# A two-block hybrid layer: the delta rule on raw keys and queries, with their norms as factors of the tokens

## What is computed

```python
qkv = silu(causal_depthwise_conv(gdn_qkv, conv_w))          # h @ w_in, first 3072 columns
qa, ka, va = split(qkv)                                      # 8 heads of 128 each
qa, ka = l2_normalize(qa), l2_normalize(ka)                  # x * rsqrt(sum(x*x) + 1e-6)
beta = sigmoid(gdn_b);  g = -exp(a_log) * softplus(gdn_a + dt_bias)
# S_t = exp(g_t) S_{t-1} + beta_t k_t (v_t - exp(g_t) S_{t-1}^T k_t)^T ;  o_t = S_t^T q_t / sqrt(128)
oa = gated_delta_rule(qa, ka, va, beta, g)
oa = oa * rsqrt(mean(oa * oa) + 1e-6)                        # per token and head
oa = oa * gdn_norm_w * silu(gdn_z)
u_a = oa @ w_branch_a
```

## Time and profile before

| what | value |
|---|---|
| time, median of 3 runs | 1242.67 us (1242.46 to 1242.71) |
| span of the profiled execution | 1240.9 us |
| PE busy | 1218.7 us, 98% |
| DVE busy | 748.4 us, 60% |
| ACT busy | 611.1 us, 49% |
| POOL busy | 95.7 us, 8% |
| mean DMA rate | 181 GB/s |
| chain that ended last | PE 90%, DVE 4%, ACT 3%, issue 1%, DMA 1% |
| conv region | 0 to 167 us |

### The profile page before, as it was taken

How to read it: one execution, slowest core, us unless ns; L and a number is a source line. 1 busy time by engine, 2 the same in 40 slices (tenths; PEclk the granted TensorE clock), 3 DMA queues, 4 the chain that set the end, 5 groups by cost and what they waited for, 6 DMA issues and landing times.

```text
span 1240.9 us, 16520 instructions
## 1 busy us (share of the span) xinstructions
PE 1218.7 (98%) x6566; PEld 1022.1 (82%) x6566; DVE 748.4 (60%) x1008; ACT 611.1 (49%) x898; POOL 95.7 (8%) x129
## 2 busy tenths in 40 slices
PE   8899999999999999999999999999999999999997
PEld 8788888888878888888888888788897778888886
DVE  5668885665576656556455555667565646565654
ACT  5566454544424556444444444564444445466443
POOL 0010000179300000000000000000000000000000
PEclk9999999999999999999999999999999999999999
DMA  8646555576644544655666585466544656464662
GB/s 258 210 140 192 165 182 159 145 214 186 184 142 131 172 129 142 215 189 171 209 181 202 190 296 199 154 208 201 168 138 151 204 170 204 125 218 163 207 206 100
DMA packets 141101, 224.00 MB, mean 181 GB/s; under 512 B 10097, under 2 KB 60849, under 8 KB 140001
## 3 DMA queue, kind: packets, MB, share of 16 engines
q1 hardware_dynamic: 138576, 212.25, 54.6%
q0 software_dynamic: 2128, 9.64, 2.2%
q10 hardware_dynamic: 320, 1.06, 0.2%
HBM read 218.20 MB, written 4.72 MB: 180 GB/s over the span
## 4 chain that ended last, share of the span: by engine, by line
PE 90%; DVE 4%; ACT 3%; issue 1%; DMA 1%; POOL 0%; SPq 0%; POOLq 0%; ACTq 0%
PE acc L1941 62%; PE acc L1920 9%; PE acc L1922 5%; PE aux L1812 3%; PE aux L2186 2%; PE acc L1873 2%; DVE lo_w L1283 1%; PE aux L2162 1%; PE acc L1932 1%; ACT hi_w L902 1%; PE aux L1992 1%; DVE cv L1397 1%; PE aux L2052 1%; DMA x_in<-in_x 0%; PE aux L2155 0%
## 5 line engine op out<-in xcount | busy, mean ns | idle before, releaser
L1283 DVE TENSOR_TENSOR lo_w<-raw_w,hi_w 128x1024 fp32r<-128x1024 f32 x379 | 462.4, 1230 | 346.5 <-ACT hi_w L902 345.1
L902 ACT ACTIVATE hi_w<-raw_w 128x1024 fp32r<-128x1024 f32 x379 | 394.7, 1057 | 267.8 <-PE acc L1941 218.8
L1941 PE MATMUL acc<-hi_w,h_both 128*128 128x512 f32 (+1 forms) x1632 | 520.2, 391 | 1.2 <-DVE lo_w L1283 0.8
L1941 PEld LDWEIGHTS acc<-hi_w,h_both 128*128 128x128 f32 x1632 | 304.7, 188 | 65.6 <-issue 3.9
L1941 PE MATMUL acc<-lo_w,h_both 128*128 128x512 f32 (+1 forms) x816 | 314.6, 385 | 0.0
L1920 PE MATMUL acc<-h_both,hi_w 128*128 128x512 f32 x576 | 204.5, 399 | 2.4 <-DVE lo_w L1283 2.4
L1941 PEld LDWEIGHTS acc<-lo_w,h_both 128*128 128x128 f32 x816 | 153.6, 188 | 28.1
L1922 PE MATMUL acc<-h_both,lo_w 128*128 128x256 f32 x576 | 160.8, 279 | 0.0
L1920 PEld LDWEIGHTS acc<-h_both,hi_w 128*128 128x128 f32 x576 | 108.2, 188 | 28.3 <-DVE lo_w L1283 1.6
L1922 PEld LDWEIGHTS acc<-h_both,lo_w 128*128 128x128 f32 x576 | 108.6, 189 | 0.1
L1941 PE MATMUL acc<-hi_w,m_hi 128*128 128x512 f32 x224 | 87.5, 390 | 0.0
(11 more groups left out here) (348 smaller groups left out, 1246.4 us busy)
## 6 DMA issues: line engine op xcount, KB each, us to landing
raw_w<-in_w_in SPq DMA_DIRECT2D x283, 512.0 KB, 3.8
raw_w<-in_w_out SPq DMA_DIRECT2D x64, 512.0 KB, 4.8
raw_w<-in_w_branch_a SPq DMA_DIRECT2D x16, 512.0 KB, 4.6
raw_w<-in_w_branch_b SPq DMA_DIRECT2D x16, 512.0 KB, 4.7
raw_w<-in_cmp_k_w SPq DMA_DIRECT2D x8, 512.0 KB, 4.3
raw_w<-in_cmp_v_w SPq DMA_DIRECT2D x8, 512.0 KB, 4.9
x_in<-in_x SPq DMA_DIRECT2D x8, 256.0 KB, 8.4
x<-in_x POOLq DMA_DIRECT2D x1, 2048.0 KB, 9.6
```

The lines of the kernel that those rows point to most:

```text
L902: act.activation(hi_w[slot][:, 0:n], raw_w[no % RAW_SLOTS][:, 0:n], ACT.Copy).then_inc(*hi_ready.event(no))
L1283: dve.tensor_tensor(lo_w[slot][:, 0:n], raw_w[no % RAW_SLOTS][:, 0:n], hi_w[slot][:, 0:n].bitcast(F32), ALU.subtract).then_inc(*lo_ready.e ...
L1941: i = pe.matmul(to[:, t, 0:group.cols], x[at], w[:, k], start=first and k == 0 and m == 0, stop=last and k == n - 1 and m == 2)
```

## The change

q and k are no longer normalised. The silu writes them straight to `q_t` and `k_t` (channels x tokens, the form that `gram` and `delta` read), `conv_back` still transposes them, but only for the sums of squares and, for k, to fill `k_tok` for the first 128 tokens. `qk_flip`, `qk_out`, the scalings on DVE and the tile `q_tok` go. With r the root factor of k per token and head, three factors are made on POOL (`k_scale`, two ticks ahead of v's tokens for half 0): `k_v` = beta r for v's tokens, `k_low` = -beta r r in place of `nbeta`, `k_beg` = beta r r exp(gcum) in place of `beg`. The norm of q and the factor 1/sqrt(128) go into the epsilon of the norm behind the delta rule (`q_eps`), as a third instruction of its root on POOL. Waits follow: v's `token_out` on DVE waits for `k_scale`, `gram` for the silus, `conv_back` for ACT's square or copy, `delta` for the copy of k.

```diff
-    at(26, "beta_gcum")
+    at(27, "k_scale", 0)
+    at(END[("conv", "k", 1, 1)] + 7, "k_scale", 1)
...
-            if part != "v":
-                at(c + 8, "qk_flip", part, h)
-                at(c + 9, "qk_out", part, h)
...
-        small = place("small", [P, 400], F32)
+        small = place("small", [P, 480], F32)
...
# POOL
             def token_out(part, h):
-                if part != "v":
-                    pool.wait_ge(*dve_did.after("ssq", part, h))
-                    root(rnorm, ssq, 1.0, ("rnorm", part, h), SCALE if part == "q" else None)
+                if part == "q":
+                    pool.wait_ge(*dve_did.after("ssq", "q", h))
+                    pool.tensor_scalar(q_eps[h], q_ssq[h], EPS / SCALE ** 2, EPS * EPS / SCALE ** 2, ALU.mult,
+                                       ALU.add).then_inc(*pool_did.event("q_eps", h))
+                if part == "k":
+                    pool.wait_ge(*dve_did.after("ssq", "k", h))
+                    root(k_r[h], k_ssq[h], 1.0, ("k_r", h))
+
+            def k_scale(h):
+                pool.wait_ge(*act_did.after("eg"))
+                pool.wait_ge(*pool_did.after("k_r", h))
+                r = tiles(k_r[h], QUAD)
+                by_v, low, by_beg = (tiles(x, HEADS)[:, :, quad(h)] for x in (k_v, k_low, k_beg))
+                link(pool.tensor_tensor(by_v, tiles(beta, HEADS)[:, :, quad(h)], r, ALU.mult))
+                link(pool.tensor_tensor(low, by_v, r, ALU.mult))
+                link(pool.tensor_tensor(by_beg, low, tiles(eg, HEADS)[:, :, quad(h)], ALU.mult))
+                pool.tensor_scalar(low, low, -1.0, None, ALU.mult).then_inc(*pool_did.event("k_scale", h))
...
             def delta_norm(h):
                 pool.wait_ge(*dve_did.after("delta_ssq", h))
-                root(rnorm, ssq, 1.0 / P, ("delta_rnorm", h))
+                pool.wait_ge(*pool_did.after("q_eps", h))
+                link(pool.tensor_scalar(rnorm, ssq, 1.0 / P, None, ALU.mult))
+                link(pool.tensor_tensor(rnorm, rnorm, q_eps[h], ALU.add))
+                pool.tensor_tensor(rnorm, rnorm, half[:, 0:NT * QUAD], ALU.pow).then_inc(
+                    *pool_did.event("delta_rnorm", h))
...
# ACT
             def conv_silu(part, h):
                 act.wait_ge(*dve_did.after("conv", part, h))
-                if (part, h) != ("q", 0):
-                    act.wait_ge(*pe_did.after("conv_back", *before_conv(part, h)))
-                act.activation(sil[:], cv[:], ACT.Silu).then_inc(*act_did.event("silu", part, h))
+                if (part, h) == ("v", 1):
+                    act.wait_ge(*pe_did.after("conv_back", "v", 0))
+                act.activation(silu_of(part, h), cv[:], ACT.Silu).then_inc(*act_did.event("silu", part, h))
...
-            def qk_out(part, h):
-                act.wait_ge(*pe_did.after("qk_flip", part, h))
...
+                if part == "k":
+                    act.activation(k_tok[:, 0, quad(h)], aux[:, 2].rearrange("p (i c) -> p i c", c=P),
+                                   ACT.Copy).then_inc(*act_did.event("k_tok", h))
...
# DVE
-                dve.tensor_scalar(nbeta, beta, -1.0, None, ALU.mult)
...
-            def beta_gcum():
-                dve.wait_ge(*act_did.after("eg"))
-                dve.tensor_tensor(beg, beta, eg, ALU.mult).then_inc(*dve_did.event("beg"))
...
             def token_out(part, h):
                 if part == "v":
                     dve.wait_ge(*pe_did.after("conv_back", part, h))
+                    dve.wait_ge(*pool_did.after("k_scale", h))
...
                 dve.wait_ge(*act_did.after("sq", part, h))
-                if (part, h) != ("q", 0):
-                    dve.wait_ge(*pool_did.after("rnorm", *before_qk(part, h)))
-                dve.tensor_reduce(tiles(ssq, QUAD), sq[:], AXX, ALU.add).then_inc(*dve_did.event("ssq", part, h))
-                dve.wait_ge(*pool_did.after("rnorm", part, h))
-                if part == "q" and h:
-                    dve.wait_ge(*pe_did.after("qk_flip", "q", 0))
-                for t in range(NT):
-                    to = q_tok[:, t] if part == "q" else k_tok[:, t, quad(h)]
-                    last = dve.tensor_tensor(to, aux[:, 2 + t].rearrange("p (i c) -> p i c", c=P),
-                                             over_cols(rnorm[:, t * QUAD:(t + 1) * QUAD]), ALU.mult)
-                last.then_inc(*dve_did.event("token_out", part, h))
+                to = (q_ssq if part == "q" else k_ssq)[h]
+                dve.tensor_reduce(tiles(to, QUAD), sq[:], AXX, ALU.add).then_inc(*dve_did.event("ssq", part, h))
...
# PE
             def conv_back(part, h):
+                reader = {"q": (act_did, "sq", "q", h), "k": (act_did, "k_tok", h), "v": (dve_did, "token_out", "v", h)}
                 for b in (2, 3):
-                    take(b, (dve_did, "token_out", part, h))
+                    take(b, reader[part])
...
-            def qk_flip(part, h):
...
             def gram(h, t):
...
-                pe.wait_ge(*act_did.after("qk_out", "k", h))
+                for part in "qk":
+                    pe.wait_ge(*act_did.after("silu", part, h))
```

More of the change, by code:

```diff
@@ L466, in build @@
         ba = bit(NT * 16)
-        beta, nbeta, g, gcum, ngcum, eg, beg = (bit(NT * HEADS) for _ in range(7))
+        beta, g, gcum, ngcum, eg = (bit(NT * HEADS) for _ in range(5))
+        k_v, k_low, k_beg = (bit(NT * HEADS) for _ in range(3))
         tail, sp0, sp1, nexp = bit(HEADS), bit(NT * HEADS), bit(NT * HEADS), bit(HEADS)
+        q_ssq, k_ssq, q_eps, k_r = ([bit(NT * QUAD) for _ in range(2)] for _ in range(4))
         ssq, rnorm = bit(NT * QUAD), bit(NT * QUAD)
@@ L664, in over_cols, with silu_of @@
             return ap.unsqueeze(2).broadcast_to([P, ap.shape[-1], m])
+        silu_to = {"q": q_t, "k": k_t}
+        def silu_of(part, h):
+            return silu_to[part][:, quad(h)] if part in silu_to else sil[:]
         conv_order = [(p, h) for h in range(2) for p in "qkv"]
@@ L774, in _, with root @@
             pool.memset(inv_t[:], 0.0).then_inc(*pool_did.event("inv_zero"))
-            def root(dst, src, scale, key, times=None):
+            def root(dst, src, scale, key):
                 n = dst.shape[-1]
                 link(pool.tensor_scalar(dst, src, scale, EPS, ALU.mult, ALU.add))
[L780 to L784, removed]
+                pool.tensor_tensor(dst, dst, half[:, 0:n], ALU.pow).then_inc(*pool_did.event(*key))
             def norm1():
@@ L873, in tail_ @@
                 root(r3[:, t:t + 1], tot[:, t:t + 1], 1.0 / D, ("r3", t))
-            steps = {"token_out": token_out, "delta_norm": delta_norm, "branch": branch, "blocks_away": blocks_away,
+            steps = {"token_out": token_out, "k_scale": k_scale, "delta_norm": delta_norm, "branch": branch, "blocks_away": blocks_away,
                      "solve": solve,
@@ L1445, in tri @@
                 link(dve.tensor_tensor(low_t[h][t][:], c["inv"][:], over_heads(upto[:]), ALU.mult))
+                if t == 0:
+                    dve.wait_ge(*pool_did.after("k_scale", h))
                 dve.tensor_tensor(attn_t[:, quad(h), t], aux[:, 2].rearrange("p (i c) -> p i c", c=P), low_t[h][t][:],
@@ L1449, in tri @@
                     o = t * HEADS + h * QUAD + i
-                    last = dve.scalar_tensor_tensor(c["wide"][:, i], aux[:, 1, i * P:(i + 1) * P], nbeta[:, o:o + 1],
+                    last = dve.scalar_tensor_tensor(c["wide"][:, i], aux[:, 1, i * P:(i + 1) * P], k_low[:, o:o + 1],
                                                     c["low_m"][:, i], ALU.mult, ALU.mult)
@@ L1490, in delta @@
                 if n == 0:
-                    dve.wait_ge(*act_did.after("eg"))
+                    dve.wait_ge(*act_did.after("k_tok", h))
                     dve.tensor_tensor(k_tok[:, 0, q4], k_tok[:, 0, q4], over_cols(tail[:, q4]), ALU.mult).then_inc(
@@ L1501, in delta @@
                     link(dve.tensor_tensor(delta_r[:], aux[:, 3].rearrange("p (i c) -> p i c", c=P),
-                                           over_cols(beg[:, o:o + QUAD]), ALU.mult))
+                                           over_cols(k_beg[:, o:o + QUAD]), ALU.mult))
                     dve.tensor_tensor(o1, aux[:, 0].rearrange("p (i c) -> p i c", c=P),
@@ L2027, in conv_back @@
                     for i in range(QUAD):
-                        last = turn(aux[:, 2 + t, i * P:(i + 1) * P], sil[:, i, t * P:(t + 1) * P])
+                        last = turn(aux[:, 2 + t, i * P:(i + 1) * P], silu_of(part, h)[:, i, t * P:(t + 1) * P])
                 last.then_inc(*pe_did.event("conv_back", part, h))
-            def qk_flip(part, h):
-                for b in (2, 3):
-                    take(b, (act_did, "qk_out", part, h))
-                pe.wait_ge(*dve_did.after("token_out", part, h))
-                for i in range(QUAD):
-                    for t in range(NT):
-                        s = q_tok[:, t, i] if part == "q" else k_tok[:, t, h * QUAD + i]
-                        o = i % 2 * SEQ + t * P
```

(4 more changed lines are left out.)

10 lines of the change are left out of this document (4 added, 6 removed).

## The result

| | before | after |
|---|---|---|
| time, median of 10 runs each | 1242.67 us (1241.12 to 1244.27) | 1245.14 us (1244.25 to 1246.4) |
| ratio | | 1.0021, 95% interval 1.0013 to 1.0029 |
| span of the profiled execution | 1240.9 us | 1243.7 us |
| PE busy | 1218.7 us | 1224.8 us |
| DVE / ACT busy | 748.4 / 611.1 us | 745.5 / 608.6 us |

What follows compares the result with a forecast made beforehand. TensorE (PE), busy 98% of the span, bounds the kernel. Flips -3.5, stall -1.5, silu wait at 109.33 -0.1 and `delta_norm` +0.3 sum to -4.8 us, so 1242.67 becomes 1237.9 us; range 1236.4 to 1239.6.

Steps and rivals of the forecast that it cites:

- At nothing: List of edits priced at no cost, such as fewer ACT copies and DVE scalings, changed waits and the larger `small`.
- Part 1: Conv region on PE: removing the 32 transposes of `qk_flip`, four groups at 0.87 us each, saves 3.5 us.
- Rival C: Each removed transpose is worth its full 272 ns, 8.7 us in place of 3.5, giving 1232.7 us; chance 0.02.
- Part 2: PE's stall at 76.67 us, waiting for DVE's split into `lo_w`, goes whole: 1.50 us saved, margin 1.6.
- Rival A: The stall at 76.67 us survives or moves, leaving a gain of 3.3 us, time 1239.4; chance 0.08.
- Part 3: The chain to `g`, which PE's `gcum` product needs, keeps up with the earlier PE: cost nothing, 1.4 us of cover.
- Part 4: PE's 0.29 us stall at 109.33 for the silu of v, half 0, stays; 0.1 us of it taken off.
- Part 5: v's tokens on DVE now wait for `k_scale`, 0.8 to 6.6 us of POOL with some 14 us available: cost 0.
- Rival D: Slower: v's tokens, half 0, wait for `k_scale` with splits queued behind; 1245.1 us at 6 us per instruction; chance 0.02.
- Part 6: `delta_norm`'s third POOL instruction costs PE 0.29 us in half 1; in half 0, if without cover, 0.3 more.
- Rival B: Conv pairs on PE may run at a quicker or slower pitch: 1237.0 to 1238.9 us; forecast with it, chance 0.86.

Runs made afterwards that it cites:

- e8: Changed kernel with `small` at 528 columns and the four groups of eight transposes put back on PE, results unread; 1242.34 us, ratio 0.9989 against before.
- e10: Changed kernel with `small` at 528 columns, and POOL's root and DVE's scaling put back for q alone, result unread; 1241.43 us, ratio 0.9984 against before.
- e2: Changed kernel with `small` at 528 columns, so tiles behind it lie 512 bytes later than in before, not 320; 1238.62 us, ratio 0.9964 against before.
- e7: Kernel before with only the weight tiles `hi_w` and `lo_w` placed 64 bytes later; 1248.39 us.
- e6: Kernel before with only `h_both` placed 64 bytes later; 1255.35 us, 12.5 above before.
- e1: Kernel before with `small` at 480 columns, so tiles behind it lie 320 bytes later, no instruction changed; 1249.95 us, ratio 1.0063.
- e4: Kernel before with `small` at 416 columns, so tiles behind it lie 64 bytes later; 1251.59 us.
- e3: Changed kernel with `small` at 496 columns, so tiles behind it lie 384 bytes later than in before; 1243.63 us.
- e9: Changed kernel with `small` at 528 columns and `delta_norm`'s root in two POOL instructions, the factor 1/128 taken out of it; 1237.94 us, ratio 0.9962 against before.
- e5: Kernel before with `small` at 464 columns, so tiles behind it lie 256 bytes later; 1242.04 us.

## Why the prediction was wrong, point by point

**The step that failed** stands under "At nothing": "`small` grows by 320 bytes a partition and shifts the tiles behind it; no row says that this costs." That no row said so is true, and it was read as a cost of nothing. Parts 4 to 6 bound what their rows don't fix from both sides; this term got no bound, and it was +7.1 us. The prediction gave 0.02 to something unseen that eats the gain, and that is what came. What could have been read: PE is 98% busy, most of it in wide products, so whatever touches each of them, by however little, had to be priced per product. At 1152 of them, 3 ns each would already have taken most of a gain of 4.8 us. The Trainium skill ("SBUF — State Buffer", Operand start alignment) has a rule on where operands start, a multiple of the element's size, and says that it is about legality and not speed. All starts here keep that rule, and still a product costs 6.7 ns more.

**Part 1, the flips: right.** The displacement of 0.87 us a group, 3.5 us in sum. After gains 2.58 us between pieces 20 and 48, where three groups went (3 x 0.87 = 2.6); e8 shows 0.88 a group and 3.1 us in all. Rival C, and with it the 275 ns of the Trainium skill ("TensorE: Matmul & The Clock Gate", Part 4) taken as a price, is out: it would have needed 8.7.

**Part 2, the stall: right.** PE waits for nothing between 55 and 80 us in after. DVE's order is the one forecast: the sum for `raw` at 65.69 (forecast 65.8) and the split at 71.62 (forecast 71.6):

```profile
64.56 1.22 DVE L1430 TENSOR_REDUCE small<-sq 128x8 f32<-128x1024 f32 x1 [0.25 <-ACT sq L1026]
65.69 0.68 DVE L1377 TENSOR_TENSOR raw<-raw,acc 128x512 f32<-128x512 f32 x1
...
71.62 1.23 DVE L1299 TENSOR_TENSOR lo_w<-raw_w,hi_w 128x1024 fp32r<-128x1024 f32 x1
```

e10 puts the cause back and PE waits again, for 1.65 us where 2.1 was expected. Rival A is out.

**Part 3, the gate chain: right.** The last step to `g` starts at 92.14 (forecast: `g` by 92.8), and PE starts its products for `gcum` at 94.42 without a wait (forecast: it asks at 94.2). DVE then waits for PE, not PE for DVE:

```profile
92.14 0.18 DVE L1329 TENSOR_TENSOR small<-small 128x16 f32<-128x16 f32 x1
...
94.96 0.18 DVE L1334 COPY small<-aux 128x16 f32<-128x16 f32 x1 [1.50 <-PE aux L2023]
```

**Part 4, the silu of v: right.** I took 0.1 off 0.29; what is left is 0.21:

```profile
106.33 0.74 PE L1816 MATMUL aux<-ident,sil 128*128 128x128 f32 x5 [0.21 <-ACT sil L1018]
```

**Part 5, `k_scale`: right.** POOL makes it from 95.84 to 98.27, and DVE's tokens of v come at 110.77 without a wait. The four instructions span 2.4 us, between the bounds of 0.8 and 6.6. The two of 0.68 and 1.07 us ran while DVE had an instruction with both inputs in SBUF, and each ended 0.07 us behind it; the other two took 0.20 and 0.24. Rival D is out.

```profile
96.12 0.68 POOL L807 TENSOR_TENSOR small<-small 128x8 f32<-128x8 f32 x1
96.88 1.07 POOL L808 TENSOR_TENSOR small<-small 128x8 f32<-128x8 f32 x1
...
110.77 1.28 DVE L1423 TENSOR_TENSOR v_tok<-aux,small 128x512 f32<-128x512 f32 x2
```

**Part 6, the third POOL instruction: right in price, wrong in count.** It costs 0.28 to 0.32 us of POOL, DVE's wait goes from 2.05 to 2.39, and PE loses 0.33. But it loses this in both halves. I saw no tightness in half 0 and counted it once; the text had the price of the other case, "0.3 more", and that is what came.

```profile
413.14 1.29 DVE L1522 TENSOR_TENSOR k_tok<-k_tok,small 128x512 f32<-128x512 f32 x2 [2.39 <-POOL small L852]
```

**Rival B, the pitch: a small part of it, on its dear side.** The mean of the pairs' medians over the 72 pair pieces is 348.3 ns in before and 349.4 in e2. Over the 256 pairs of pieces 16 to 47 that would be 0.3 us less gained. In before 22 of the 72 pieces have a median of 347 or less, in e2 10. What sets it stays open: no tile of these products moved.

**The sum again.** e2 has the edited part alone: -0.11 up to piece 15, -4.56 to piece 48 (forecast -5.1: flips, stall and the 0.1 at v's silu), +0.33 and +0.33 at the two `delta_norm`s; together -4.0, its end. The forecast of -4.8 misses it by 0.5 for flips, stall and pitch, and 0.3 for half 0. With +7.1 for the tiles this is +3.1, against +2.8 in the spans and +2.5 in the medians. That the edited part lands at -4.0 against -4.8 is no luck: each of its terms is seen in the traces by itself. One slip in the chances: B, A and C all lie below 1240.2 and have 0.96 together, where "faster" was given 0.93.

## What to carry to other kernels

When a change makes a buffer larger, look at every tile that is placed behind it, and ask which hot instruction reads it; round the size up so that the tiles keep their places modulo 256 bytes, which here cost 48 elements and brought back 7 us. Where one engine is nearly full, price what touches all of its instructions in nanoseconds before what touches four of them in microseconds. And when a result has the wrong sign, lay the starts of a repeated unit of work side by side: it says in one table where the forecast held and where it was eaten. It also takes out what differs ahead of the edit: at piece 15 the twelve profiles already lie up to 2.4 us apart.

## What the runs showed of the hardware that I had not expected

**The place of a tile in SBUF sets the pace of the wide products.** One 128x512 product follows another by 226.7 ns where the stationary tile lies a multiple of 256 bytes from its place in before, by 232.6 to 233.3 where it is off by 64, 320 or 384; with the moving one off by 64 it is 228.9. The weight loads are shown at 0.19 us in every one of these kernels, so the profile doesn't say which part of a product is longer:

```profile
L1945 PEld LDWEIGHTS acc<-hi_w,m_hi 128*128 128x128 f32 x224 | 42.1, 188 | 10.0
```

Nor is it a rule for all products: those of q0, 256 columns wide with a weight block of `hi_w` or `lo_w` stationary, follow each other by 120 ns in before, by 113 with the weights off by 64 bytes (e7) and by 118 with `h_both` off (e6), so they get quicker. All of these are products of tiles that the kernel declares as F32R. Those of tiles declared as F32 keep their step: the 128-column transposes of tiles behind `small` 109 ns, and the 256-column products of `mk_t` and `mq_t` 216 ns, in before, e1 and e4 alike. What happens inside PE or on the way from SBUF isn't shown; nor are shifts under 64 bytes, nor whether each start counts or the distance between the two tiles.

**The granted clock can fall for a moment behind an idle stretch, or not.** In the profile of after PE was idle for 2.53 us up to 43.41, and then ran 3.4 us at half its clock, 1.2 GHz; the products followed each other by 0.65 us a pair. In before the idle time there was 2.58 us, and the clock stayed at 1.00. The first fence is PE's timeline in after, the second the window of 40 to 50 us (length, then busy us and count of PE, PEld, DVE, ACT and POOL, granted clock, DMA share, GB/s):

```profile
43.41 1.00 PE L2250 MATMUL aux<-r_diag,ones 128*128 128x256 f32 x2 [2.53 <-DVE r_diag L1366]
...
44.84 0.63 PE L1924 MATMUL acc<-h_both,hi_w 128*128 128x512 f32 x1
...
45.49 0.63 PE L1924 MATMUL acc<-h_both,hi_w 128*128 128x512 f32 x1
```

```profile
40.00:50.00 10.00, 7.47 (x34) 6.16 (x33) 7.79 (x12) 6.05 (x10) 0.89 (x2) 0.83 0.75 219
```

In after this cost nothing in the end: the 1.1 us that before waits for `lo_w` at piece 15 weren't waited for, and the two kernels start that piece within 0.10 us. Of the twelve profiles, eight show such a drop of 3.4 us between 42 and 49 us, and before, e2, e3 and e9 don't; the idle stretch ahead of it was 2.58 us in e2 too, and 2.09 in e5, which has the drop. Four (e4, e6, e8, e9) show one between 990 and 1010 us. After, e2 and e3 run the same instructions. So it comes and goes between executions that are alike up to there, and at about 1.5 us it is a reason not to read differences of one microsecond between two single profiles from their ends.
